# Second attention: ScalarE copies the stick scores to SBUF behind the absolute value

## What is computed

```python
def stick_breaking_mixer(qkv):
    q, k, v = qkv[:, :, 0], qkv[:, :, 1], qkv[:, :, 2]
    def block(n):                       # 128 queries at a time, 4 blocks
        z = jnp.einsum('bqhd,bshd->bhqs', qb, k).astype(jnp.float32) * scale
        causal = kpos[None] < t[:, None]
        log_beta = jax.nn.log_sigmoid(z)
        log_fail = jnp.where(causal, jax.nn.log_sigmoid(-z), 0.0)
        after = lax.cumsum(log_fail, axis=3, reverse=True) - log_fail
        a = jnp.where(causal, jnp.exp(log_beta + after), 0.0)
        return jnp.einsum('bhqs,bshd->bqhd', a.astype(dt), v)
```

## Time and profile before

| | |
|---|---|
| Runs, median of 3 | 1174.12 us (1172.09 to 1176.47) |
| Profiled execution, its own time | 1174.21 us |
| its span, first to last instruction | 1172.4 us |
| mean granted TensorE clock | 0.977 |
| PE busy | 1114.2 us (95%) |
| DVE busy | 641.7 us (55%) |
| ACT busy | 424.9 us (36%) |
| POOL busy | 529.8 us (45%) |

### The profile page before, as it was taken

The page is one execution under the profiler, slowest core; times in us unless marked ns, Lnnn a source line. Parts: engine busy times, 40 slices in busy tenths (PEclk is TensorE's granted clock), DMA queues, the critical chain, the costliest instruction groups (busy, mean ns, idle before and its releaser), DMA issues.

```text
span 1172.4 us, 16124 instructions
## 1 busy us (share of the span) xinstructions
PE 1114.2 (95%) x5801; PEld 954.3 (81%) x5801; DVE 641.7 (55%) x1131; ACT 424.9 (36%) x852; POOL 529.8 (45%) x525
## 2 busy tenths in 40 slices
PE   6999999999989999999988987789999999999998
PEld 5788888888779888898888877788878888888887
DVE  6869777677567646485666586735641321321321
ACT  5373668363446532114553565423020110110110
POOL 0000000000443327989454177308976776777772
PEclk9999999999999999999999897699999999999999
DMA  6322322413211002323221000102322223223221
GB/s 249 125 88 90 110 88 93 141 54 126 90 54 37 20 18 73 126 90 127 72 73 55 18 2 18 55 1 91 125 91 97 101 90 108 90 93 104 89 89 54
DMA packets 27280, 97.18 MB, mean 83 GB/s; under 512 B 3024, under 2 KB 3408, under 8 KB 27088
## 3 DMA queue, kind: packets, MB, share of 16 engines
q1 hardware_dynamic: 27216, 96.32, 24.6%
HBM read 94.21 MB, written 2.10 MB: 82 GB/s over the span
## 4 chain that ended last, share of the span: by engine, by line
PE 76%; DVE 12%; ACT 5%; issue 4%; POOL 1%; DMA 1%; SPq 0%; DVEq 0%; POOLq 0%; ACTq 0%
PE bank L1236 21%; PE bank L1238 21%; PE bank L1237 21%; PE bank L788 4%; PE bank L751 3%; PE bank L768 3%; DVE arena L1967 1%; DVE wl L1918 1%; ACT wh L1597 1%; PE bank L810 1%; DVE arena L1021 1%; DMA x<-x_in 1%; POOL wl L1189 0%; DVE arena L2318 0%; DVE arena L939 0%
## 5 line engine op out<-in xcount | busy, mean ns | idle before, releaser
L1185 POOL TENSOR_TENSOR hold<-hold 128x2 f32<-128x2 f32 x117 | 29.3, 251 | 531.2 <-PE bank L1238 531.2
L1236 PE MATMUL bank<-xh,wh 128*128 128x512 f32 x568 | 226.5, 399 | 12.0 <-DVE xl L1887 9.4
L1237 PE MATMUL bank<-xl,wh 128*128 128x512 f32 x568 | 222.0, 391 | 0.0
L1238 PE MATMUL bank<-xh,wl 128*128 128x512 f32 x568 | 221.9, 391 | 0.0
L1236 PE MATMUL bank<-yh,wh 128*128 128x512 f32 x520 | 203.5, 391 | 2.0 <-DVE yl L2323 1.5
L1238 PE MATMUL bank<-yh,wl 128*128 128x512 f32 x520 | 202.6, 390 | 0.0
L1237 PE MATMUL bank<-yl,wh 128*128 128x512 f32 x520 | 202.5, 389 | 0.0
L1189 POOL TENSOR_TENSOR wl<-raw,wh 128x512 fp32r<-128x512 f32 x117 | 175.2, 1498 | 0.0
L1188 POOL TENSOR_TENSOR wl<-raw,wh 128x512 fp32r<-128x512 f32 x117 | 157.1, 1343 | 9.7
L1236 PEld LDWEIGHTS bank<-xh,wh 128*128 128x128 f32 x568 | 107.1, 189 | 35.1 <-issue 11.6
L1186 POOL TENSOR_SCALAR wh<-raw 128x1024 fp32r<-128x1024 f32 x117 | 126.6, 1082 | 0.0
(11 more groups left out here) (260 smaller groups left out, 1856.6 us busy)
## 6 DMA issues: line engine op xcount, KB each, us to landing
raw<-weight_units SPq DMA_DIRECT2D x173, 512.0 KB, 3.4
x<-x_in SPq DMA_DIRECT2D x4, 512.0 KB, 7.6
out_fm<-x SPq DMA_DIRECT2D x8, 256.0 KB, 2.0
arena<-tables SPq DMA_DIRECT2D x1, 1024.0 KB, 10.6
par<-params SPq DMA_DIRECT2D x1, 166.0 KB, 2.4
arena<-swa_table SPq DMA_DIRECT2D x1, 128.0 KB, 11.5
ident<-identity SPq DMA_DIRECT2D x1, 64.0 KB, 8.9
```

The costliest lines, as they stand in the source:

```text
L1185: pool.tensor_tensor(hold[:], hold[:], hold[:], ALU.add).then_inc(held, 1)
L1236: pe.matmul(out, lh, rh, start=start, stop=False)
L1237: pe.matmul(out, lh, rl, start=False, stop=False)
L1238: return pe.matmul(out, ll, rh, start=False, stop=stop)
```

## The change

ACT copies a stick's scores from their bank into the group's probability buffer, straight behind the Abs. That copy is now the last read of the bank and frees it. DVE's sum and difference read the copy; the difference works in place. The wait for the transposes of the group four back moves from DVE's difference to ACT's Abs, and ACT's wait for the difference two sticks back goes. A new semaphore, `sdiff`, tells ACT's last Exp that the difference is done. No other instruction changes its place.

```diff
@@ soft1 (ACT) @@
                         act.wait_ge(s["scores"], st + 1)
-                        if n3 >= 6:
-                            j = [j for j in range(i) if is_stick(j)][-2]
-                            act.wait_ge(*strip_read(groups[j]["strip0"]))
+                        if i >= 4:
+                            act.wait_ge(s["pt_ready"], groups[i - 4]["chunks"][-1][0] + 1)
 
                         act.activation(lt, score_bank(st)[:, 0:w], ACT.Abs).then_inc(s["soft1"], 1)
+                        act.activation(pr[:, 0:w], score_bank(st)[:, 0:w], ACT.Copy).then_inc(strip_read(st)[0], 1)
                         act.wait_ge(s["soft1"], n3 + 1)
@@ soft2 (ACT) @@
-                    act.wait_ge(*strip_read(g["strip0"]))
+                    act.wait_ge(s["sdiff"], stick_count(i) + 1)
                     pr = probs_of(i)[:, 0:g["w"][0]]
                     act.activation(pr, pr, ACT.Exp).then_inc(s["sprobs"], 1)
@@ mask2 (DVE) @@
-                    z = score_bank(g["strip0"])[:, 0:w]
                     dve.wait_ge(s["soft1"], 3 * stick_count(i) + 3)
 
-                    link(dve.scalar_tensor_tensor(out=lt, in0=z, scalar=0.0, in1=lt, op0=ALU.max, op1=ALU.add))
+                    link(dve.scalar_tensor_tensor(out=lt, in0=pr, scalar=0.0, in1=lt, op0=ALU.max, op1=ALU.add))
                     link(dve.tensor_tensor_scan(lt[:, ::-1], ones[:, 0:1].to_broadcast([P, w]), lt[:, ::-1],
                                                 0.0, ALU.mult, ALU.add))
-                    if i >= 4:
-                        dve.wait_ge(s["pt_ready"], groups[i - 4]["chunks"][-1][0] + 1)
-                    dve.tensor_tensor(pr, z, lt, ALU.subtract).then_inc(strip_read(g["strip0"])[0], 1)
+                    dve.tensor_tensor(pr, pr, lt, ALU.subtract).then_inc(s["sdiff"], 1)
```

More of the change, by code:

```diff
@@ L420, in two_block_kernel @@
                 "scores", "read0_", "read1_", "read2_", "read3_", "soft1", "probs", "pt_ready", "pt_even", "pt_odd",
-                "o_done", "fin5_", "fin6_", "sprobs", "pairT", "pair_done", "esum")}
+                "o_done", "fin5_", "fin6_", "sprobs", "sdiff", "pairT", "pair_done", "esum")}
         block = ctx.enter_context(nc.Block())
```

## The result

| | before | after |
|---|---|---|
| Runs, median | 1173.11 us of 4 (1171.89 to 1176.47) | 1186.74 us of 4 (1186.02 to 1188.27) |
| Profiled execution | 1174.21 us | 1186.62 us |
| Mean granted TensorE clock | 0.977 | 0.971 |

The account below looks back on a forecast made before the run. PE, busy 95%, bounds the kernel, following DVE in three stretches between 558 and 765 us. On 1174.21 us, 0.4 + 0 + 0 + 3.8 + 1.9 = +6.1 us gave 1180.3 us, range 1173 to 1188 (8 in 10).

Parts of the forecast that it names:

- rival 1: DVE and POOL take strict turns, each new operation in the DVE-bound stretches held 1.26 us; 1186.6 to 1190 us, chance 0.15.
- the four sticks: Sums starting at 603, 642, 726 and 734 us: 8 operations held 0.48 us each by POOL, +3.8 us (0 to 10.1).
- the six sticks: 673 to 725 us: 12 operations held 0.48 us, a third reaching PE, +1.9 us (0 to 5.8).
- the first stall: PE's 1.69 us bank wait at 568.58 us: gain at most 1.7, loss at most 0.8, taken as 0.
- Copies: ACT's 24 copies mostly covered by idle time; one 256-wide copy on the path near 684.02 us, +0.4 us.
- the new wait: ACT's wait ahead of the Abs for the transposes of the group four back, priced at 0.
- the three later bank releases: Bank waits at 605.23, 643.41 and 737.44 us: PE meets DVE's own queue next, gain 0 of 6.9 us.
- Rival 3: The banks decide: all 8.6 us of PE's bank waits are won; 1165.6 us, chance 0.07.
- Bare duration: Difference at 512 columns: 691 ns with a PSUM operand, 692 with both in SBUF while POOL idles; worth 0.
- Rival 4: SBUF operand 65 ns cheaper, 3 us for DVE over 48 operations, 0.5 reaching PE; 1173.7 us, chance 0.03.
- Rival 2: Holds fall into DVE's idle time or replace others, bank waits only change name; 1172.5 to 1177 us, chance 0.25.
- The signs: Sum and difference medians above 0.49, maxima above 1.2 us beside POOL; DVE busier by 4 to 10 us, ACT by 10.

Follow-up runs that it names:

- copies-only kernel: Against the changed kernel: ACT's copies and moved wait kept, but DVE's sum and difference read the bank again and the difference frees it; 1175.87 us, 1.0026.
- pair with light splits: Copies alone and the changed kernel, each with POOL splitting only 8 of 1024 columns per unit from the second attention on; 1161.76 and 1161.67 us.

## Why the prediction was right, and which terms were off

The direction, the cause and the range held; 1186.74 us lies inside 1173 to 1188, but 6.4 us above the forecast, at the lower end of rival 1's times. That the sum for the attention, 6.1 us, comes within 4.2 us of the 10.3 measured is in part luck: the term for the four sticks had two errors that nearly cancel, the one for the six sticks was met by the clock and not by holds, and two effects, the first stall and the clock, stood in it at nothing. Point by point:

- *Copies, +0.4, and the new wait, 0.* Together 0.26%, 3.1 us, when alone; I priced one place of 24. The wait ahead of the Abs shows little: ACT idles there 2.4 us in two places for PE's transposes, where before it idled 2.3 us in two places for PE's mask. In the copies-only kernel it is 4.8 us in four. How the 3.1 us divide between copies and wait was not tried. The row of the Abs after, then before:

```profile
  PE bank L768: 2.4, 2
```

```profile
  PE bank L754: 2.3, 2
```

- *Waits taken away, 0; the three later bank releases, 0 of 6.9.* Right. All four waits went and were replaced by waits at the next transpose, product or scores, as their successors in PE's timeline show, and the pair with light splits finds no value in the release either. Rival 3 falls.
- *Bare duration, 0.* Right: minima of 293 and 291 ns. Rival 4 and the rule behind it (the Trainium skill, "VectorE: DVE Perf Modes", section on the TRN2 errata) are not borne out. The scan that reads and writes the bank shows no penalty either: 428 ns, against 425 with SBUF operands and light splits.
- *Holds in the four sticks, 8 x 0.48 = +3.8.* The size of a hold was the number most wrong. The four sticks grew by 7.6 us, 0.95 for each new operation. I took 0.48 from L2323 in the MLP, an operation that stands alone and meets POOL's instruction at any phase. Sum, scan and difference stand one behind another, and each meets the beginning of POOL's next instruction. The rows of L2280 and L2281 had shown that, and I had given it to rival 1. But I also let all of it reach PE, and of the 7.6 us only 4.2 did (ledger, lines 2, 3 and 6; 4.5 counted as PE's idle time). The two errors nearly cancel.
- *Six sticks of 673 to 725 us, +1.9.* The stretch (line 5) grew by 2.0 us, and that is luck. There were 3.7 us of holds instead of 5.8, and PE's idle time grew by 0.1 us and not by a third of them. The rest is PE busy 1.9 us longer at a clock of 0.84 instead of 0.87; in its second trace the changed kernel has 0.88 there, and the stretch is 0.6 us longer than before.
- *First stall, 0.* Wrong by 2.1 us (line 1), 1.7 of it PE standing still. I set a gain of 1.7 against a loss of at most 0.8. The gain was not to be had, since ACT and DVE behind it were late. The two sticks beside POOL's last splits, those of 560.6 and 566.8 us before, grew by 4.4 us; the first of them I had not counted.
- *PE's clock, not in the sum.* Of the 10.3 us, 6.5 are PE standing still and 3.8 are PE slower at the same matmuls, at a clock of 0.86 instead of 0.88. How much of the 3.8 the change causes stays open: with the difference alone on the copy PE stands still for 38.7 us in the same stage, nearly as long as in the changed kernel, and is busy 185.6 us, less than before.
- *Rival 1,* strict turns: in mechanism the better forecast, in time by luck. Its 1186.6 us had 10.1 us at PE for the four sticks, where 4.2 arrived. I held against it that other holds would shrink. They did (L2280 and L2281, 0.74 and 1.19 us before, are L2277 and L2278 after, 0.20 and 0.21 us, POOL having stopped by then), but DVE's busy time in the stage still rose by 13.8 of the sticks' 16.5 us. *Rival 2,* hidden, falls by the result.
- *The signs.* The medians of sum and difference are 0.56 and 0.69 us and their maxima 1.42 and 1.57, as said. DVE is 13.7 us busier, above the 4 to 10 given, and ACT 4.7 and not 10.

The medians differ by 13.6 us and the attention by 10.3. The rest can be placed. The profiled executions differ by 12.4: 2.0 lie before the attention, 0.1 behind it. Of the 2.0, 0.5 are there when PE's wait of 2.32 us near 339 us ends (338.78 and 339.26 us), and 1.5 come from the clock right behind it (last section). The other 1.2 us are the distance of the two profiled executions from their medians. The 2.1 us before and behind the attention lie where the change touches nothing.

## What to carry to other kernels

Before an operand is moved from PSUM to SBUF to free a bank, look whether the operation then has both inputs in SBUF and whether GpSimd works beside it: here that took the 128-wide difference from 291 to 839 ns, and the early bank gained nothing. Where operations of that kind follow one another, price each at nearly a whole GpSimd instruction (0.95 us here, of about 1.3), not at the mean of a lone one (0.48); and price apart what of it reaches the engine that sets the end (here 4.2 of 7.6 us beside the splits, next to none beside the doublings). And before pricing the end of a wait, name what the waiting engine stands at next; all four waits removed here came back one step later. A single stretch of one execution can differ by 2 us through the clock alone, so compare its idle time too.

## What was not expected of the hardware

- Some 1.4% of the kernel's time (18 us by the medians) goes with POOL's splits beside other work: with them cut to 8 columns DVE's busy time falls from 641.7 to 571.3 us with the same instructions. The page of the kernel before with light splits:

```profile
PE 1103.2 (96%) x5801; PEld 943.6 (82%) x5801; DVE 571.3 (50%) x1131; ACT 424.4 (37%) x852; POOL 174.3 (15%) x525
```

- POOL's instructions carry a large fixed part: a subtraction of 128 columns takes 443 ns at the shortest and 517 in the mean, one of 512 takes 1260 at the shortest; four times the width for 2.8 times the shortest time.
- PE's busy time fell with them from 1114.2 to 1103.2 us at a mean granted clock of 0.989 instead of 0.977, for the same matmuls. Less idle time and a higher clock went together here, but not in every pair of traces: see PE's clock in the section before.
- The granted clock also differs between executions where no work does. Behind the same idle time of 2.32 us at 339 us, the window 338.5 to 345.5 us had a clock of 0.76 in the changed kernel and 1.00 in the one before; 29 instructions of PE began in it against 44. Other kernels with an unchanged first half showed either.
